# Gate tables of a PEER layer: one-hot matmuls against indirect scatters into cleared tables

## The reference

```python
s1 = jnp.einsum('mhd,hnd->mhn', q[:, :, 0], sub_keys[0]).astype(jnp.float32)   # 8 heads, 128 keys a side
s2 = jnp.einsum('mhd,hnd->mhn', q[:, :, 1], sub_keys[1]).astype(jnp.float32)
v1, i1 = lax.top_k(s1, PEER_TOPK)                                              # 16 of 128, each side
v2, i2 = lax.top_k(s2, PEER_TOPK)
cand_s = (v1[..., :, None] + v2[..., None, :]).reshape(M, PEER_HEADS, PEER_TOPK * PEER_TOPK)
cand_i = (i1[..., :, None] * PEER_KEYS + i2[..., None, :]).reshape(M, PEER_HEADS, PEER_TOPK * PEER_TOPK)
top_s, top_pos = lax.top_k(cand_s, PEER_TOPK)                                  # 16 of 256
idx = jnp.take_along_axis(cand_i, top_pos, axis=-1)
gate = jax.nn.softmax(top_s, axis=-1)
...
u = expert_u[idx_b]
act = jax.nn.gelu(jnp.einsum('mhkd,md->mhk', u, x_b).astype(jnp.float32))
return jnp.einsum('mhk,mhkd->md', act * g_b, expert_v[idx_b].astype(jnp.float32))
```

## Time and profile before

| | |
|---|---|
| runs | 4390.5, 4393.67, 4403.39 us |
| median | 4393.67 us |
| profiled execution | 4389.36 us, span 4387.6 us |
| busy, share of the span | PE 93%, PEld 77%, DVE 62%, POOL 45%, ACT 35% |
| DMA | 693.34 MB, mean 158 GB/s |
| granted clock of TensorE, mean | 0.959 |

### The profile page before, as it was taken

One profiled execution on the slowest core, in us unless ns is written; L12 is line 12 of the kernel. 1 busy time (PEld: TensorE's weight loads), 2 busy tenths in 40 slices (PEclk: granted clock), 3 DMA queues, 4 the chain that ended last, 5 costly groups with the idle time before them and its releaser, 6 DMA issues.

```text
span 4387.6 us, 64423 instructions
## 1 busy us (share of the span) xinstructions
PE 4089.7 (93%) x19814; PEld 3376.1 (77%) x19814; DVE 2734.7 (62%) x5853; ACT 1549.1 (35%) x2469; POOL 1969.2 (45%) x1210
## 2 busy tenths in 40 slices
PE   7978888999999999999889888889999999999997
PEld 5776666888888887888766766668888888878886
DVE  4456323176868678888754562232768686688886
ACT  3424333333333333333334243433333333333333
POOL 4340333344343427777443413333443434377773
PEclk9988888999999999999999888899999999999999
DMA  3200121144353539999622012211444535399995
GB/s 125 87 1 20 67 96 55 68 145 141 131 196 126 202 126 338 333 338 343 225 98 87 1 30 76 78 68 68 144 138 151 177 144 185 138 343 339 341 333 219
DMA packets 232649, 693.34 MB, mean 158 GB/s; under 512 B 30544, under 2 KB 75696, under 8 KB 224816
## 3 DMA queue, kind: packets, MB, share of 16 engines
q1 hardware_dynamic: 134448, 444.88, 28.6%
q0 software_dynamic: 45888, 138.58, 8.2%
q10 hardware_dynamic: 52160, 107.98, 6.7%
HBM read 588.53 MB, written 102.81 MB: 158 GB/s over the span
## 4 chain that ended last, share of the span: by engine, by line
PE 55%; issue 26%; POOL 8%; DVE 3%; ACT 2%; PEld 1%; POOLq 1%; DVEq 1%; ACTq 1%; DMA 0%; PEldq 0%
PE PS L478 15%; PE PS L479 15%; PE PS L480 15%; POOL u_lo L1935 6%; POOL w_lo L1874 2%; PE PS L935 1%; PE PS L657 1%; PE PS L643 1%; PE PS L850 1%; ACT junk L972 1%; PE PS L895 1%; PE PS L661 1%; PE PS L532 1%; PE PS L472 1%; PE PS L860 1%
## 5 line engine op out<-in xcount | busy, mean ns | idle before, releaser
L1935 POOL TENSOR_TENSOR u_lo<-u_raw,u_hi 128x1024 fp32r<-128x1024 f32 x256 | 623.4, 2435 | 971.7 <-ACT u_hi L1284 971.7
L478 PE MATMUL PS<-h_hi,u_hi 128*128 128x512 f32 x2048 | 806.1, 394 | 2.2 <-POOL u_lo L1935 1.1
L479 PE MATMUL PS<-h_lo,u_hi 128*128 128x512 f32 x2048 | 797.4, 389 | 0.0
L480 PE MATMUL PS<-h_hi,u_lo 128*128 128x512 f32 x2048 | 797.2, 389 | 0.0
L1874 POOL TENSOR_TENSOR w_lo<-wring,w_hi 128x512 fp32r<-128x512 f32 (+1 forms) x352 | 467.4, 1333 | 600.0 <-ACT w_hi L991 596.1
L478 PE MATMUL PS<-v_hi,g_hi 128*128 128x512 f32 x1536 | 601.5, 392 | 22.8 <-DVE g_lo L1831 22.8
L1284 ACT ACTIVATE u_hi<-u_raw 128x1024 fp32r<-128x1024 f32 x256 | 271.2, 1060 | 947.9 <-PE PS L480 889.6
L479 PE MATMUL PS<-v_lo,g_hi 128*128 128x512 f32 x1536 | 600.3, 391 | 0.0
L480 PE MATMUL PS<-v_hi,g_lo 128*128 128x512 f32 x1536 | 600.1, 391 | 0.0
L1365 ACT ACTIVATE v_hi<-v_raw 128x1024 fp32r<-128x1024 f32 x256 | 271.6, 1061 | 560.8 <-PE PS L480 551.0
L1953 POOL DMA_INDIRECT v_row<-in_expert_v,row_index x256 | 381.6, 1491 | 165.3 <-DVE X L1841 107.4
(11 more groups left out here) (330 smaller groups left out, 6928.0 us busy)
## 6 DMA issues: line engine op xcount, KB each, us to landing
u_raw<-in_expert_u SPq DMA_DIRECT2D x256, 512.0 KB, 3.3
v_raw<-in_expert_v SPq DMA_DIRECT2D x256, 512.0 KB, 6.8
wring<-in_weights SPq DMA_DIRECT2D x42, 2048.0 KB, 8.5
acts_dram<-act_ring ACTq DMA_DIRECT2D x256, 256.0 KB, 2.0
saved<-acts_dram SPq DMA_DIRECT2D x64, 768.0 KB, 11.3
gates_dram<-gstage ACTq DMA_DIRECT2D x16, 2048.0 KB, 7.6
gates<-gates_dram SPq DMA_DIRECT2D x64, 512.0 KB, 6.5
crow_all<-crow_dram ACTq DMA_DIRECT2D x8, 512.0 KB, 6.0
```

Source lines behind the costliest of these rows:

```text
L478: mm(bank_ap, a_hi, b_hi, start=first, stop=False)
L479: mm(bank_ap, a_hi, b_lo, start=False, stop=False)
L480: return mm(bank_ap, a_lo, b_hi, start=False, stop=final)
L1935: g.tensor_tensor(u_lo[:, slot, :], u_raw[:, slot, :], u_hi[:, slot, :].bitcast(f32), ALU.subtract).then_inc(ulo_ready, 1)
```

## The change

- The one-hot rows, their matmuls and transposes, the copies, `gstage` and the stores are gone. All three tables lie in `gates_dram`.
- Each pick becomes one 4-byte write. VectorE works out its place (`gate_place`), and for each head adds up the gates of all picks of the same token with the same place (`same_place`: a comparison, a product and a reduce of 2048 elements each), so that equal picks write equal values. GpSimd issues 16 indirect transfers a head, 128 elements each, and before the next head's waits on `gates_scattered` until all before have landed.
- The tables are cleared in each layer by three transfers from `zeros`, 1 KB rows, on SP's queue between the mixer's weights and the output projection's. ScalarE waits for their landing before it overwrites that area.
- The low parts of `expert_u` move from GpSimd to VectorE (`low_u`), placed between the picking's steps. The rings grow from two to four; the second pair of slots is loaded after the scores' stage. The gathered tile is picked last (`PICK_ORDER`).
- In the values stage VectorE's product is one instruction over three tables, SP loads three tables a time, and the first load waits for all scatters.

```diff
+U_RING = 4
+LOWS_TO_BEST, LOWS_OF_DENSE, LOWS_OF_GATHERED = 9, 30, 15
+PICK_ORDER = (1, 2, 3, 0)
...
-    gates_dram = nc.dram_tensor("gates_dram", (NG - 1, P, NEXP_HI, P), f32, kind="Internal").ap()
...
+        u_raw_0, u_hi_0, u_lo_0 = area("u_raw", 10240, 2, DC * P), area_r("u_hi", 12288, 2, DC * P), area_r("u_lo", 14336, 2, DC * P)
+        u_raw_2, u_hi_2, u_lo_2 = area("u_raw2", 26624, 2, DC * P), area_r("u_hi2", 28672, 2, DC * P), area_r("u_lo2", 30720, 2, DC * P)
+
+        def ring_of(first, second, slot):
+            return first[:, slot] if slot < 2 else second[:, slot - 2]
...
         digits = area("digits", 18048, 2, P, dt=u32)
-        gstage = area("gstage", 26624, NEXP_HI, P)
+        gate_place, gate_value = area("gate_place", 32768, NG, P, dt=u32), area("gate_value", 33152, NG, P)
+        zeros = area("zeros", 32384, 2 * P)
...
+        gate_ring = [area("gates0", 43008, NG, QUAD * P), area("gates1", 33600, NG, QUAD * P)]
...
+                sp.wait_ge(zeros_ready, 1)
+                for t in range(NG):
+                    sp.dma_start(gates_dram[t].rearrange("p i c -> p (i c)").rearrange("p (r n) -> p r n", n=2 * P),
+                                 zeros.rearrange("p (o n) -> p o n", o=1).to_broadcast([P, NEXP_HI // 2, 2 * P])).then_inc(gates_zeroed, 16)
...
+                for slot in range(2):
+                    load_u(slot, slot)
+                sp.wait_ge(stage_done, 4 * (S_PQ + 1))
+                for slot in range(2, U_RING):
+                    load_u(slot, slot)
+                with nc.sync.Fori(1, NEXP_HI // U_RING) as j:
+                    for slot in range(U_RING):
+                        load_u(j * U_RING + slot, slot)
...
+                sp.wait_ge(index_ready, 1)
+                for r in range(QUAD):
+                    load_v(r, r)
                 for slot in range(2):
                     sp.wait_ge(act_saved[slot], 16 * QUAD // 2)
+                sp.wait_ge(gates_scattered, l * (16 * NG * P) + 16 * NG * P)
                 load_gated(0, 0)
...
+                with nc.tensor.Fori(0, NEXP_HI // U_RING) as j:
+                    for slot in range(U_RING):
+                        expert_acts(j * U_RING + slot, slot)
...
+                act.wait_ge(gates_zeroed, 16 * NG)
...
+                def acts_round(j, first=False, final=False):
+                    for slot in range(U_RING):
+                        if not final:
+                            split_u(j * U_RING + (slot + U_RING), j + 1, slot)
+                        gelu_saved(j * U_RING + slot, j * 2 + slot // 2, slot, first and slot < 2)
+
+                def gate_exps(i):
+                    act.wait_ge(gate_diff, i + 1)
+                    fn(picked[:, 2, :], picked[:, 2, :], ACT.Exp).then_inc(gate_exp, 1)
 
...
+                for slot in range(2, U_RING):
+                    split_u(slot, 0, slot)
+                rounds = [(2 + i * LOWS_OF_DENSE + LOWS_TO_BEST + U_RING - 1) // U_RING for i in range(NT)]
+                acts_round(0, first=True)
+                at = 1
+                for i in range(NT):
+                    with nc.scalar.Fori(at, rounds[i]) as j:
+                        acts_round(j)
+                    gate_exps(i)
+                    at = rounds[i]
+                with nc.scalar.Fori(at, NEXP_HI // U_RING - 1) as j:
+                    acts_round(j)
+                acts_round(NEXP_HI // U_RING - 1, final=True)
...
                 qk_items = [conv[:, i, :] for i in range(8)] + [raw[:, 16 + i, 3:RW] for i in range(8)]
+                v.memset(zeros, 0.0)
+                dve.drain().then_inc(zeros_ready, 1)
...
-                for t in range(NT):
+                n_low = 2
+                for i, t in enumerate(PICK_ORDER):
+                    start = n_low
                     for k in range(16):
                         top16(scores[:, t, k * P:(k + 1) * P], rest[:, k % 4, :], top[:, k, :], topi[:, k, :])
+                        if k % 3 == 2:
+                            low_u(n_low)
+                            n_low += 1
                     dve.drain()
...
+                        if h % 2 == 1:
+                            low_u(n_low)
+                            n_low += 1
+                    assert n_low == start + LOWS_TO_BEST
...
+                        low_u(n_low)
                         v.tensor_reduce(picked[:, side, :], side_hot, AX.X, ALU.add)
                         dve.drain()
-                    dve.wait_ge(gate_exp, t + 1)
+                        low_u(n_low + 1)
+                        n_low += 2
+                    dve.wait_ge(gate_exp, i + 1)
...
                     v.tensor_tensor(gate, gate, along(rinv[:, 0:PH], TOPK), ALU.mult)
...
+                    v.tensor_scalar(digitf[:, 0, :], picked[:, 0, :], float(P), own_place, ALU.mult, ALU.add)
+                    dve.drain()
+                    v.scalar_tensor_tensor(digitf[:, 0, :], picked[:, 1, :], float(NEXP_HI * P), digitf[:, 0, :], ALU.mult, ALU.add)
+                    dve.drain()
+                    v.tensor_scalar(gate_place[:, t - 1, :], digitf[:, 0, :], float((t - 1) * P * NEXP_HI * P), None, ALU.add)
+                    same_place = scores[:, t, :].rearrange("p (k n) -> p k n", n=P)
+                    for h in range(PH):
+                        slots = slice(h * TOPK, (h + 1) * TOPK)
+                        v.tensor_tensor(same_place, along(digitf[:, 0, slots], P), over(digitf[:, 0, :], TOPK), ALU.is_equal)
+                        dve.drain()
+                        v.tensor_tensor(same_place, same_place, over(picked[:, 2, :], TOPK), ALU.mult)
+                        dve.drain()
+                        low_u(n_low)
+                        n_low += 1
+                        v.tensor_reduce(gate_value[:, t - 1, slots], same_place, AX.X, ALU.add)
+                        dve.drain().then_inc(picks_ready, 1)
+                        if h < PH - 1:
+                            low_u(n_low)
+                            n_low += 1
...
                 stage_end(dve, l, S_PICK)
                 v.tensor_copy(place_f[:], row_index[:])
                 dve.drain()
@@ -1819,12 +1805,8 @@
                             dve.wait_ge(saved_loaded[half], g * 16 + 16)
                         dve.wait_ge(wlo_ready, g * PAIR + (k + 1))
                         wt, saved = wt_ring[:, k % 2, :], saved_ring[half][:, r, :]
-                        last = (NG - 1) * P
-                        v.tensor_tensor(wt[:, 0:last].rearrange("p (t c) -> p t c", c=P),
-                                        saved[:, 0:last].rearrange("p (t c) -> p t c", c=P),
...
                 stage_end(pool, l, S_PQ)
-                with g.Fori(1, NEXP_HI // 2) as j:
-                    for slot in range(2):
-                        split_u(j * 2 + slot, slot)
+
+                gates_by_place = gates_dram.rearrange("t p i (c o) -> (t p i c) o", o=1)
+                for t in range(NG):
+                    for h in range(PH):
+                        pool.wait_ge(picks_ready, t * PH + h + 1)
+                        done = t * PH + h
+                        if done:
+                            pool.wait_ge(gates_scattered, l * (16 * NG * P) + 16 * TOPK * done)
+                            pool.sem_inc(scatter_room, 1)
```

More of the change, by code:

```diff
@@ L351, in trunk_kernel @@
         row_gathered = [sem(f"row_gathered{r}") for r in range(GATHERS)]
-        gates_out = lsem("gates_out")
         act_saved = [lsem("act_saved0"), lsem("act_saved1")]
-        u_loaded = [lsem("u_loaded0"), lsem("u_loaded1")]
+        u_loaded = [lsem(f"u_loaded{r}") for r in range(U_RING)]
         v_loaded = [lsem(f"v_loaded{r}") for r in range(QUAD)]
@@ L905, in expert_acts @@
                         cs = slice(c * P, (c + 1) * P)
-                        last = parts_product(PS[:, slot, :], u_hi[:, slot, cs], u_lo[:, slot, cs], h_hi[:, c, :], h_lo[:, c, :],
+                        last = parts_product(PS[:, slot, :], u_hi(slot)[:, cs], u_lo(slot)[:, cs], h_hi[:, c, :], h_lo[:, c, :],
                                              c == 0, c == DC - 1)
@@ L1312, in _ @@
                 stage_end(act, l, S_PQ)
-                for slot in range(2):
-                    acts_step(0, slot, first=True)
-                with nc.scalar.Fori(1, U_FIRST // 2 - 1) as j:
-                    for slot in range(2):
-                        acts_step(j, slot)
-                act.wait_ge(gate_diff, 1)
-                fn(picked[:, 2, :], picked[:, 2, :], ACT.Exp).then_inc(gate_exp, 1)
-                for slot in range(2):
-                    acts_step(U_FIRST // 2 - 1, slot)
@@ L1440, in _ @@
                 dve.sem_inc(wlo_ready, 2)
+                dve.sem_inc(ulo_ready, U_RING)
                 norm(0, X, NT, "mix", hT)
@@ L1736, in _, with low_u @@
                 split_x(XP_PQ, h_lo, hT, h_hi)
+                def low_u(n):
+                    dve.wait_ge(uhi_ready, n + (U_RING + 1))
+                    slot = n % U_RING
```

(8 more changed lines are left out.)

168 lines of the change are left out of this document (34 added, 134 removed).

## The result

| | before | after |
|---|---|---|
| median of the runs | 4394.06 us (4390.5 to 4403.39) | 4319.24 us (4316.76 to 4321.42) |
| span of the profiled execution | 4387.6 | 4314.6 |
| PE, DVE, POOL busy | 93%, 62%, 45% | 91%, 62%, 52% |
| DMA | 693.34 MB | 727.24 MB |

The ratio is 0.9826, 95% interval 0.9809 to 0.9843: 75 us faster. 4315 was predicted.

The account below looks back on a forecast made before the run. TensorE was taken to bound the expert acts' stage before, GpSimd's scatters after. Terms of -45.4 + 3 + 2 + 2 = -38 us a layer, -77 in two, gave 4312 or 4316, taken as 4315; range 4240 to 4460.

Parts of the forecast that it names:

- Part 1 and 2: Expert acts: spreading leaves TensorE, low parts move to VectorE; TensorE's stage 698 + 8 + 2 = 708 us.
- Part 3: Expert acts: 384 scatters on GpSimd end at 740 us, 32 after TensorE, and bound the stage: 740.6 against 786.
- Part 4: Clearing the tables on SP's queue slows the fetch of `gb`: 0 to 10 us, taken as 3 a layer.
- Part 5: Values stage: third table's traffic 2 us, first tables asked for later another 2 us, per layer.
- The sum: Whole kernel: -45.4 + 3 + 2 + 2 = -38 us a layer, -77 in two layers; 4315 taken.
- That the scatters hide: Rival, expert acts: scatters end by 708 us, TensorE bounds, -73 us a layer, kernel 4247; chance 0.22.
- Slow landing: Rival: GpSimd's batch waits above 3.9 us eat the whole gain; at 6.4 kernel 4512; landing or spacing above break-even 0.19.
- Every issue blocked: Rival: reduce and MAX8 on VectorE also block scatter issues; GpSimd ends at 901 us, kernel 4640; chance 0.04.
- VectorE held up by scatters: Rival: some 70 two-input operations a tile each 0.5 us late; stage 805 us, kernel 4445; chance 0.03.

Follow-up runs that it names:

- late_clear: Changed kernel, with the three clearing transfers behind the first pair of projection weights, waiting for the end of the stage that uses `gb`: 4317.45 us.
- own_tables: Changed kernel, each head scattering into its own tables, landing waits only between tiles, seven eighths of the gates left out: 4254.9 us.
- one_input: Changed kernel, both 2048-element products of a head's gate sum replaced by one-operand reduces, equal picks not summed: 4248.09 us.
- pool_first: Changed kernel, with the first 17 low parts of `expert_u` made on GpSimd instead of VectorE: 4305.72 us.
- combo: Changed kernel with accumulated one-instruction gate sums, first 17 low parts on GpSimd, no drain after the scatters, clearing behind the use of `gb`: 4229.95 us.

## Why the prediction was right

*Part 1 and 2, TensorE's stage.* Predicted 708, measured 709.2. Its waits in the stage are 8.8 us (6.5 for low parts, 2.3 for high parts), against 8 + 2. Not in the sum was the clock: behind the longest wait, of 3.18 us at 897.9, the granted clock is 0.5 for 3.4 us, and matmuls start 0.43 us apart instead of 0.23, which is 1.6 us by an estimate from these rows.

*Part 3, the scatters as the bound.* Predicted end 740 us, measured 745.8. By terms, after the first head (96.8 us, predicted 97): issue with its 0.30, 384 x 1.503 = 577 against 588; landings 68.2 - 23 x 0.30 = 61 against 55, the mean wait 2.97 us for about 2.6; and three stops of together 9 us that no row of before shows. In the second layer the chain ends at 739.7, with landings of 63.3 in place of 68.2 us, so 6 us lie between two passes of the same code. The mechanism of the earlier trace rows held: where VectorE makes the sums, the scatters of a batch are spaced 1.65 to 1.87 us on average in the two layers, elsewhere 1.26 to 1.6. Not in the sum was what follows the last scatter: 3.8 us until GpSimd lets go. So 749.6, not 740.6; the second layer has 743.5.

*Part 4, the clearing.* Predicted +3 a layer, measured +3.1 at `gb`; late_clear showed it. Where the first acts begin +1.0 is left, and the whole kernel shows no difference that is clear of the spread. The clearing holds SP for 50.5 us and each transfer lands 31 to 56 us after its issue; nothing else was found to wait.

*Part 5, the values stage.* Predicted +4, measured -0.5. The third table went by at 342 GB/s with TensorE as busy as before, and from 1700 to 1800 us at 365, more than the 355 I had taken as the highest: it cost nothing. From the first matmul of the fifth group of values to the last matmul TensorE takes 505.7 us in both kernels. The late first tables do delay the first matmul, 7.2 us behind VectorE's first instruction instead of 3.8, and this is paid back, as the prediction expected of most of it: TensorE's waits behind its first matmul fall from 6.3 to 2.4 us.

*The sum.* Acts stages -78.8 for -90.8, the rest +5.8 for +14: -73.0 in spans against -77. The two misses, 12 us too hopeful in the acts and 8 too careful around them, nearly cancel, and that the number came within 4 us is luck to that extent. Of the +6.7 ahead of the second layer's acts 4.5 are TensorE's own time at a lower granted clock, as the windows above show; they belong to no term.

*The rivals.* That the scatters hide failed by 37 + 4 us; own_tables and one_input show that it lacked one of two costs only, and 4248 and 4255 are near the 4247 worked out for it. The prediction gave the best landing 0.9 us a batch of what this rival needed; no landing came under 1.99 us, 1.7 without the 0.30, which is 0.6 less than the 2.3 of the sum. Slow landing: the longest wait is 5.2 us, but the mean 2.97 stays under the break-even of 3.9. Every issue blocked: refuted by the 0.96 us scatters beside reduces. VectorE held up by scatters: refuted by the maximum of 1286 ns. That GpSimd's tensor operations do hold VectorE (pool_first) is another matter than its transfers' issues.

## What to carry to other kernels

A stream of indirect transfers on GpSimd is priced by three rows: the issue (about 1.26 us here, and longer wherever VectorE reads two operands), the landing at each ordering wait, and when the first input is ready, since the chain has no slack and 90 us of late start cost 144 us in two layers. When it ends just behind the bound, shorten what it waits for on the other engine first: short one-pass sums beside it were worth 65 us and compute the same, the waits' removal 64 with most gates left out. Read a gain inside the stage where it is claimed, and in both layers: stretches of unchanged code moved by several microseconds here, in part through the granted clock. And order the producer so that the stream's work comes first and the work that feeds something else last.

## What was not expected of the hardware

GpSimd stops for 3 to 6.6 us without a visible cause after 113, 226 and 339 scatters of each layer (3.94, 3.02, 3.01; then 3.88, 3.02, 6.64 us), and at the same counts in own_tables (3.04, 3.08, 5.02), combo (3.06, 3.02, 3.02) and all the other experiments. It goes by the number of scatters, not by time or by VectorE; among the gathers of the values stage it doesn't come, nor in the kernel before. In the changed kernel a DMA packet of the kind `instruction` falls into only one of the six stops, so the trace does not show the loading of code as their cause. The cause stays open; it costs 9 us in the first layer and 13 in the second.

The landing of a batch of 16 transfers of 4-byte writes takes 2.0 us at best after the last issue and 5.2 at most.
